# Fused softmax front in the first layer's prompt attention, and its sample attention as a pipeline over requests

## What is computed

```python
o_cmp = softmax(q kc^T * scale) vc                      # compressed blocks of 64 keys
o_sel, _ = attend_gathered(qi, ks, vs, valid)           # selected blocks, all of them here
o_win, _ = attend_dense / banded_attention(...)         # window of 512
def attend(q, k, v, mask):
    s = where(mask, (q k^T) * hd ** -0.5, NEG)
    m = max(s); p = exp(s - m); l = sum(p)
    return (p / l) v
o_nsa = gate[0] * o_cmp + gate[1] * o_sel + gate[2] * o_win
```

## Time and profile before

| | us |
|---|---|
| median of 3 runs | 3399.26 (3393.23 to 3401.03) |
| the profiled execution, its own time | 3398.85 |
| its span, first to last instruction | 3397.0 |

### The profile page before, as it was taken

The page is one execution under the profiler, slowest core; times in us unless marked ns, Lnnn a source line. Parts: engine busy times, 40 slices in busy tenths (PEclk is TensorE's granted clock), DMA queues, the critical chain, the costliest instruction groups (busy, mean ns, idle before and its releaser), DMA issues. The chain is left out here.

```text
span 3397.0 us, 47818 instructions
## 1 busy us (share of the span) xinstructions
PE 2811.2 (83%) x19979; PEld 2531.4 (75%) x19979; DVE 1343.7 (40%) x2611; ACT 904.8 (27%) x1596; POOL 915.0 (27%) x427
## 2 busy tenths in 40 slices
PE   6766579577767889999786997688899878799998
PEld 5643379564446889999775787577899657799997
DVE  6664330138833242223365345543310444332224
ACT  3211121014402242122423113312222443421212
POOL 2221022014400353333432222222322001443331
PEclk9866789569956989999888888888999989899999
DMA  4100222624011212222221001100222135222221
GB/s 142 53 0 25 81 54 82 108 103 210 1 38 36 71 59 85 87 77 73 79 67 52 27 5 60 40 27 15 62 86 81 68 85 150 63 85 77 87 84 56
DMA packets 217604, 232.89 MB, mean 69 GB/s; under 512 B 40972, under 2 KB 186700, under 8 KB 216782
## 3 DMA queue, kind: packets, MB, share of 16 engines
q1 hardware_dynamic: 202686, 225.20, 21.8%
q10 hardware_dynamic: 14704, 4.63, 0.6%
HBM read 207.86 MB, written 48.35 MB: 75 GB/s over the span
## 5 line engine op out<-in xcount | busy, mean ns | idle before, releaser
L270 POOL TENSOR_TENSOR WRr<-WR,WH 128x2048 fp32r<-128x2048 f32 (+3 forms) x98 | 442.7, 4518 | 957.4 <-ACT WH L258 957.4
L2025 PE MATMUL PS<-HHr,WRr 128*128 128x288 f32 x1152 | 343.9, 299 | 0.0
L410 PE MATMUL PS<-HHr,WH 128*128 128x288 f32 (+1 forms) x928 | 278.7, 300 | 52.0 <-PEq L96 52.0
L410 PE MATMUL PS<-YTr,WRr 128*128 128x288 f32 x1024 | 303.8, 297 | 0.0
L258 ACT CAST WH<-WR 128x2048 fp32r<-128x2048 f32 (+3 forms) x98 | 180.3, 1841 | 384.7 <-DMA WR<-in_mlp_w 190.2
L410 PE MATMUL PS<-YTr,lt_WX 128*128 128x288 f32 x1408 | 281.7, 295 | 0.0
L410 PE MATMUL PS<-HTr,WH 128*128 128x288 f32 (+1 forms) x928 | 277.8, 299 | 0.0
L410 PE MATMUL PS<-HHr,WRr 128*128 128x288 f32 (+1 forms) x928 | 277.8, 299 | 0.0
L410 PE MATMUL PS<-WH,HHr 128*128 128x256 f32 (+3 forms) x760 | 219.9, 289 | 20.1 <-PEq L96 20.1
L2025 PE MATMUL PS<-HHr,WH 128*128 128x288 f32 x768 | 228.6, 298 | 9.4 <-POOL HTr L2013 8.6
L410 PEld LDWEIGHTS PS<-YTr,lt_WX 128*128 128x128 f32 x1408 | 227.1, 188 | 0.1
(11 more groups left out here) (641 smaller groups left out, 6460.1 us busy)
## 6 DMA issues: line engine op xcount, KB each, us to landing
WR<-in_mlp_w SPq DMA_DIRECT2D x64, 1024.0 KB, 5.3
WR<-in_cd_w_in SPq DMA_DIRECT2D x34, 1024.0 KB, 5.4
out_dil_s<-in_cache_dil_kv SPq DMA_DIRECT2D x2, 7936.0 KB
WR<-in_ab_w_in SPq DMA_DIRECT2D x10, 1024.0 KB, 5.3
past_rows<-in_cache_nsa_kv SPq DMA_DIRECT2D x16, 256.0 KB, 3.4
YT<-in_state_ssm ACTq DMA_DIRECT2D x16, 256.0 KB, 4.7
out_ssm_s<-YT SPq DMA_DIRECT2D x16, 256.0 KB
WR<-in_ab_w_in SPq DMA_DIRECT2D x16, 256.0 KB, 4.3
```

The costliest lines, as they stand in the source:

```text
L270: pool.tensor_tensor(K.WRr[:, n % RING, 0:used], K.WR[:, n % RING, 0:used], high_slot(K, i, used).bitcast(F32), ALU.subtract).then_inc(K.l ...
L410: last = pe.matmul(out, a, b, start=(n == 0), stop=(n == 3 * len(terms) - 1))
L2025: last = pe.matmul(out, a[:, k, c], h[:, k, x], start=(n == 0), stop=(n == 3 * KT - 1))
```

## The change

Prompt attention: mask, maximum and scaling become one `tensor_tensor_reduce` per half, which reads PSUM and a mask tile `MK` in SBUF, writes `-scale*(s + mask)` into `E` and its minimum into `mx`. The exponential then runs in place on `E`. Scores wait for `nm_ready` of two units before and no longer for the exponentials; the front waits for the turn of three units before. The gate is no longer multiplied into the reciprocal but is a second scalar of both products. SP first issues 16 loads of the requests' old rows (into free parts of `HF` and `HT`) and six small ones of new and compressed values (into `KV`), then the bulk copies. POOL, after its 64 products, clears a part of `KV` and writes the block-diagonal queries of all requests there.

Sample attention: each request has 256 old keys and only its own 8 new ones. Keys are copied by ACT. The compressed scores of all requests are taken together at the start, with one exponential. The two softmaxes of a request have the fused front; the compressed weights are copied between them, so that 5 transposes and one small value product cover all. Values are products of 64 columns for each group. PE's list for a step is keys of s+1, scores of s, values of s-2, turn of s-1.

```diff
 def nsa_prompt(...)
             def _(sp):
+                for b in range(NB):
+                    sp.dma_start(request_rows(K, b)[:, 0], K.past[b, :, 256:512].rearrange("(n p) c -> p n c", p=P))\
+                      .then_inc(K.request_in, 16)
+                    sp.dma_start(request_rows(K, b)[:, 1], K.nsa_win[0, b].rearrange("(n p) k g d -> p n (k g d)", p=P))\
+                      .then_inc(K.request_in, 16)
+                for h in range(2):
+                    b0, c = 4 * h, (256, 512)[h]
+                    sp.dma_start(KV[0:NS, 0:4, c:c + P], K.o_nsa_win_s[0, b0:b0 + 4, PAST - NS:, 1].rearrange("b s g d -> s b (g d)"))                      .then_inc(K.request_in, 16)
+                    sp.dma_start(KV[NS:NS + SBLK, 0:4, c:c + P], VCS[:, b0:b0 + 4]).then_inc(K.request_in, 16)
+                    sp.dma_start(KV[NS + SBLK:2 * NS + SBLK, 0:4, c:c + P],
+                                 K.o_nsa_kv_s[0, b0:b0 + 4, :, 3].rearrange("b s g d -> s b (g d)")).then_inc(K.request_in, 16)
...
                     if u >= 2:
-                        pe.wait_ge(exp_done, 2 * (u - 1))
+                        pe.wait_ge(nm_ready, 2 * (u - 1))
...
-                    act.wait_ge(nm_ready, u + 1)
                     if u >= 3:
-                        act.wait_ge(turned, u - 2)
-                        act.wait_ge(rg_ready, u - 2)
+                        act.wait_ge(p_even, u - 2)
+                        act.wait_ge(p_odd, u - 2)
                     for g in range(2):
-                        act.activation(E[:, u % 3, g, 0:L], K.PS[:, 2 * (u % 2) + g, 0:L], ACT.Exp, scale=SCALE,
+                        act.wait_ge(nm_ready, 2 * u + g + 1)
+                        act.activation(E[:, u % 3, g, 0:L], E[:, u % 3, g, 0:L], ACT.Exp, scale=-1.0,
...
-                    pool.wait_ge(rg_ready, u + 1)
-                    pool.tensor_scalar(E[:, u % 3, 0, 0:L], E[:, u % 3, 0, 0:L], sm[:, u % 3, 0:1], None,
-                                       ALU.mult).then_inc(p_even, 1)
+                    pool.wait_ge(r_ready, u + 1)
+                    pool.tensor_scalar(E[:, u % 3, 0, 0:L], E[:, u % 3, 0, 0:L], sm[:, u % 3, 0:1], gate(u, 0),
+                                       ALU.mult, ALU.mult).then_inc(p_even, 1)
+                pool.memset(KV[:, 0:4, 0:256], 0.0).then_inc(zeroed, 1)
+                pool.wait_ge(zeroed, 1)
+                for g in range(2):
+                    r = slice(g * HD, (g + 1) * HD)
+                    for b in range(NB):
+                        t0 = SEQ + b * NS
+                        pool.tensor_copy(request_queries(KV, b)[r, g * HD:(g + 1) * HD].rearrange("p (i m) -> p i m", i=NS),
+                                         QT[r, :, t0:t0 + NS].rearrange("p m i -> p i m"))
...
                     if u >= 3:
-                        dve.wait_ge(exp_done, 2 * (u - 2))
-                    diag = K.PS[:, b:b + 2, i * P:L]
-                    do(dve.tensor_tensor(diag, diag, bc(K.CM[:], 1, 2), ALU.add))
-                    do(dve.tensor_reduce(mx[:, u % 3, :], K.PS[:, b:b + 2, 0:L], AX.X, ALU.max))
-                    dve.tensor_scalar(mx[:, u % 3, :], mx[:, u % 3, :], -SCALE, None, ALU.mult).then_inc(nm_ready, 1)
+                        dve.wait_ge(turned, u - 2)
+                    for g in range(2):
+                        dve.tensor_tensor_reduce(E[:, u % 3, g, 0:L], K.PS[:, 2 * (u % 2) + g, 0:L], MK[:, SEQ - L:], -SCALE, -NEG,
+                                                 ALU.add, ALU.min, mx[:, u % 3, g:g + 1]).then_inc(nm_ready, 1)
...
-                    do(dve.reciprocal(sm[:, u % 3, :], sm[:, u % 3, :]))
-                    dve.tensor_tensor(sm[:, u % 3, :], sm[:, u % 3, :],
-                                      GT[:, i, :].rearrange("p (j g m) -> p j g m", j=3, g=2)[:, j + 1, :, m], ALU.mult).then_inc(rg_ready, 1)
...
+                    dve.reciprocal(sm[:, u % 3, :], sm[:, u % 3, :]).then_inc(r_ready, 1)
...
+                    dve.tensor_scalar(E[:, u % 3, 1, 0:L], E[:, u % 3, 1, 0:L], sm[:, u % 3, 1:2], gate(u, 1),
+                                      ALU.mult, ALU.mult).then_inc(p_odd, 1)
...
 def nsa_sample(...)
+                def scores(b):
+                    pe.wait_ge(k_copied, b + 1)
+                    if b >= 2:
+                        pe.wait_ge(nm_ready, 2 * (b - 1))
+                    t0 = SEQ + b * NS
+                    for j, (new, old) in enumerate(((0, NS), (PAST, 0))):
+                        bank = 2 + 2 * (b % 2) + j
+                        pe.matmul(K.PS[:, bank, new:new + NS], request_queries(KV, b), KTT[:, j, t0:t0 + NS], start=True, stop=True)
+                        pe.matmul(K.PS[:, bank, old:old + PAST], request_queries(KV, b), KTb[:, b % 2, j * PAST:(j + 1) * PAST],
+                                  start=True, stop=True).then_inc(s_mm, 1)
...
+                pe.wait_ge(K.request_in, 16 * (2 * NB + 6))
+                turn_keys(0)
+                compressed()
+                for s in range(NB + 2):
+                    if s + 1 < NB:
+                        turn_keys(s + 1)
+                    if s < NB:
+                        scores(s)
+                    if s >= 2:
+                        values(s - 2)
+                    if 1 <= s <= NB:
+                        turn(s - 1)
...
+                for s in range(NB + 2):
+                    if s >= 2:
+                        weights(s - 2)
+                    if s < NB:
+                        front(s)
+                    if s == 0:
+                        compressed_front()
+                    if s == 1:
+                        compressed_back()
+                    if 1 <= s <= NB:
+                        back(s - 1)
+                    if s >= 2:
+                        y(s - 2)
```

233 lines of the change are left out of this document (119 added, 114 removed).

## The result

| kernel | median us | ratio to before | 95% interval |
|---|---|---|---|
| before | 3397.22 (3393.23 to 3401.03, 4 runs) | | |
| after | 3269.89 (3266.08 to 3276.91, 4 runs) | 0.9628 | 0.9606 to 0.9649 |

The profiled execution of the kernel after took 3276.91 us, 7 above its median, with a span of 3275.1.

What follows compares the result with a forecast made beforehand. The prediction took a ring through POOL to bound the prompt stage and a chain with one request in it, at low clock, the sample stage. Terms -25 + 2 - 78 = -101 us took 3399.3 to 3298 us, range 3275 to 3335.

Steps and rivals of the forecast that it cites:

- (b): Prompt stage: the gate as second scalar on POOL and DVE changes nothing; POOL's bounds were unchanged and doubled.
- (a): Prompt stage: fused front and dropped gate product shorten the ring by 0.78 us, the pace by 0.39, saving 25 us.
- (c): End of the prompt stage: POOL's memset and 16 copies stand out and add 2 us, between 0 and 7.5.
- rival B: Prompt stage: POOL's second scalar costs 50 to 100% more, kernel at 3318 to 3339 us; chance 0.17.
- (d): Prefetch: SP's 22 transfers delay the bulk copies by some 30 us, covered by some 35 us; effect nothing.
- (e): Sample stage: PE sets a pace of 4.4 us at full clock; 52 us instead of 130, saving 78.
- the factor of 1.08: Prompt stage's 198 us against the ring's 183; also applied to the sample stage to reach 52 us.
- A: Sample stage: the clock stays low, kernel at 3323 us; chance 0.13.
- C: Prompt stage: DVE was the bound and the ring opens to PE's own work, kernel at 3283 us; chance 0.15.
- D: Prompt stage: the wait is replaced by another and the gain is 5 us, kernel at 3318; chance 0.09.
- E: Prompt stage: fusing saves nothing, only the gate product's 6 us are gained, kernel at 3317 us; chance 0.02.
- S: Prompt stage: POOL leaves its present path with two pointer scalars and becomes the bound; 3451 us at fourfold; chance 0.02.

Runs made afterwards that it cites:

- b2: Kernel after with the prompt stage's old computation, keeping prefetch, POOL's tail and new sample stage: 3301.78 us, ratio 0.9727.
- b3: Kernel after with the fused front, but the gate product separate again and one scalar on POOL and DVE: 3286.39 us, ratio 0.9679.
- f1: b3 with a column of ones as second pointer scalar on POOL's multiplication: 3277.82 us, ratio 0.9649.
- b1: Kernel before with a column of ones as second pointer scalar on POOL's prompt multiplication: ratio 1.0003, prompt stage 196.5 us.
- c2: Kernel before with ACT's copy of turned weights moved between the two exponentials of the prompt stage: ratio 0.9995, prompt stage 196.2 us.
- e1: Kernel before with both b1's second POOL scalar and c2's move of ACT's copy: 3382.99 us, ratio 0.9964, prompt stage 183.3 us.
- d2: Kernel after with the sample stage's requests one after the other on PE and DVE: 3314.22 us, ratio 0.9761, sample stage 85.1 us.
- b4: Kernel after with the old front, keeping the gate as second scalar on POOL and DVE: 3300.59 us, ratio 0.9717.
- e2: b3 with ACT's copy of turned weights moved between the two exponentials: prompt stage 173.5 us in one execution.
- e3: Kernel after with DVE's sample-stage multiplications of the request before put ahead of the current fronts: 3263.46 us, ratio 0.9611.

## Why the prediction was right or wrong

The direction and the size of the sample stage's gain were right; the time was not, and in each stage what sets the pace was read only in part. The 28 us of the miss are 10 in the prompt stage (33.2 less for 23), 7 in the sample stage (85.1 less for 78), 4 outside both, and 7 because the profiled execution, from which the stages are read, was 7 us slower than the median. The step that failed is (b): it put POOL's second scalar at nothing, and the instruction became 0.5 us shorter, worth 9 to 10 us of the kernel. The 10 us of the prompt stage are, by the rounds, 9.0 from there, 4 too many put for (a), 2 put for (c) that didn't come, and 3 of the low clock and the ends.

**(a) The fused front, 25 us.** The price of the instruction was right (0.28 to 0.69 us, 488 ns on average), and so was the gain to a few us: b2 to b3 gives 21.8 for the front alone where its 0.58 us were worth 64 x 0.29 = 18.6, f1 to after 2.5 for the gate product where its 0.20 us were put at 6.4; at full clock they are 19.9 and 1.0. The reason was only half right. The waits were read as one ring, through POOL, because 71.9 us of PE's wait stood at its name. ACT's and DVE's ends of 25 us were in the same row and were taken for a remainder. POOL's name carries the time up to its own end also where ACT would have kept PE as long, as b1's rows show. ACT's ring was of nearly equal length, b1, c2 and e1 show. The front is in both, which is why its shortening counted in full. (One reading is off: the earlier trace rows give 0.74 us from the scores of 256 keys to the next entry, not 0.71; it moves nothing.)

**(b) The gate as second scalar: the step that failed.** The bounds were "unchanged" and "doubled", with nothing below: no reason was given that a second operation can't make an instruction shorter, and 1275 ns became 778. With the fused front this is worth 10.3 us (b3 to f1), 9.0 at full clock. That 10.3 is also the miss of the whole stage is chance, as the other terms cancel. The rule of the Trainium skill that was weighed there, "GPSIMD Engine Reference", 3.1 (a body of at most two operations is bound by its port), spoke for no extra cost, and there was none; that the second operation makes the instruction shorter it doesn't say. The objection, that the rows show 3.0 ns an element and not the page's rate, was right and was used for rival B alone, when it was as good a sign that the one-scalar form may be the slow one. Why it is slower no run shows. The two-scalar form still takes 1.36 ns an element.

**(c) POOL's tail, 2 us.** The memset took 0.95 us (1.2 put), the copies 290 ns on average (350 put), all 17 from 902.5 to 907.4. DVE's last copy of y ends at 907.5, so nothing stands out; PE begins 1.61 us after its last product. b2's rounds at full clock are those of before (23.75 and 23.76), so tail and prefetch cost the stage nothing that shows.

**(d) The prefetch, nothing:** right as a cost; the DMA share is down to 0.03 from 860 on, ahead of the 880 reckoned. The first products wait 1.61 us at the barrier and for no transfer. Its worth was given no term: PE's 8.5 us of waits for loads went down to that.

**(e) The sample stage, 52 us:** 46.9 came out, boundary included. The pace of 4.4 us was 3.97 at full clock and right in size by accident: PE's value products were put at 1.28 us and take 0.88 with the new keys' (eight of 64 columns in 0.62), its scores were put at 1.2 and take 1.4 (0.51 for 256 old keys, not the 0.355 taken over from the prompt stage; 0.15 for 8 new ones, not 0.25), and PE was taken to set the pace when a ring through scores, DVE's second front and its multiplications did. That branch was worked out at 1.7 us "beside values"; it came to 1.46, but the turn it ends in is followed by keys and scores before the next one can begin, and the sum 0.60 + 0.43 + 1.48 + 1.46 us (930.43, 931.03, 931.46, 932.94, 934.40) closes a ring that is longer than PE's list. Where the clock stood at 0.57 two turns are 5.5 us apart (919.94 and 925.49), where 7.9 was put for 0.50; with the pipeline off and 0.50 throughout it is 10.3. The low clock of the start cost 6.4 us where 5 were put; the factor of 1.08 taken over from the prompt stage had no reason here and is another 4. The pace (2.6 too much) and the factor (4) less the clock (1.4 too little) make the 5 us by which 46.9 is under 52; the other 2 are the old stage, 132.0 and not 130.

**The rivals.** A (clock low throughout, 3323): the mean was 0.79, no; d2 shows what it would have been for a stage in series. B was wrong in its sign. C's 3283 was nearer than the forecast, but DVE's order was not the bound: e1 has DVE's old list and 183.3 us. D's mechanism, the wait moves on to the copies, is just what b1 and b4 show for the scalar alone; for the fused front it doesn't hold, since the front lies in both rings. E had no part. S was right that POOL behaves otherwise with two scalars, and wrong in the direction.

**Outside the two stages** 5.0 us went, and the start moved by 1.35. The time after the sample stage is 2322.3 to 2326.7 us in the four kernels with its old form and 2318.1 to 2327.4 in the fifteen with the new one (mean 2320.8). That is mostly spread; whether some us of it belong to the change wasn't tested.

## What to carry to other kernels

Where an instruction waits for several engines, the wait's name in the profile may hide a second one: here 71.9 us stood at POOL, and shortening POOL alone brought 2.6. Before pricing a wait, look in the timeline when each of the others was released; of two rings of nearly the same length, shortening one gives little and both give more than the sum (2.6, 2.7 and 13.8 us). An unseen form of an instruction needs a bound below as well as above. In a pipelined stage check for each engine's list whether an item that the next engine waits for stands behind one that it doesn't need: moving one line gave 4.6 us, and the width of the products nothing that shows. Compare stages at the same clock: by stage times alone e2's edit seemed worth 3.0 us and e3's 11.0, at the same clock they are 0.9 and 4.6.

## What the hardware showed

- POOL's TENSOR_SCALAR on fp32 takes 3.0 ns an element with one multiplication and 1.36 with two, whether the second operand is a pointer or an immediate: 1848, 1038 and 964 ns at 512 columns.
- On ACT a copy or exponential starts 0.09 us after the accumulator read before it has started (833.51 to 833.60 before the second exponential, 834.17 to 834.26 before the copy, in the kernel before), though the read is listed with 0.19 us.
- The same instructions at the start of the sample stage ran at a granted clock of 1.00 in one kernel and 0.54 to 0.77 in another, 38.9 and 45.3 us; with one request at a time PE stayed at 0.50 for 80 us.
